# The first expert step's rows picked by one-hot matrix products instead of a gather, in a two-layer transformer kernel

## The chip, the cores and the metric

The kernel runs on one core of a Trainium2 chip, in one launch, all arithmetic in float32. The metric is the device time of one execution in microseconds (us). Before the change it is 2463.87 us, the median of three runs (2461.8 to 2465.14). One further execution was recorded by the hardware profiler; all rows below come from it.

PE is the matrix engine (TensorE), DVE the vector engine, ACT the scalar engine, POOL the GpSimd engine, SP the engine that only issues transfers. Each runs its own instruction stream; they wait for each other through counting semaphores.

## What is computed

Two layers over 1024 latent tokens of width 1024. Layer 0 mixes tokens by attention and a gated linear recurrence, layer 1 by a short convolution. Both end in the same mixture of experts: a router picks, for each token, a group and two of that group's 8 experts (32 experts in all), and every token goes through its two experts. Cut to what matters here:

```
tokens = modulate(h_lat, m[3], m[4])            # h * (1 + scale) + shift, per column
g_sel  = argmax(tokens @ wg + bg)               # 4 groups
top_i  = top_2(tokens @ we + be, inside g_sel)  # 2 of 8 experts
y      = (silu(x @ w1[e]) * (x @ w3[e])) @ w2[e]     # for each token x and each of its experts e
y_tok  = sum over the two experts of weight * y
h_lat  = layer_norm(alpha * h_lat + m[5] * y_tok)
```

`w1` and `w3` are 1024 x 512, `w2` is 512 x 1024: 6 MB per expert in float32, 192 MB per layer.

## The kernel before

**Steps and places.** How many tokens an expert gets is known only at run time. The kernel sorts the experts by load on the chip, with experts 0 and 1 always put first, and gives each a fixed *place* with a fixed capacity (`CAPS`). The places are packed into `NB` = 22 *steps* of up to 128 rows (`STEPS`). Step 0 holds places 0 and 1, which are experts 0 and 1 with 64 rows each, so its weights are known before routing; step 1 holds places 16 and 17, whose experts are known only from the routing result (`order`). Assignments beyond the capacities go to a run-time loop after the 22 steps, which stays empty if there are none.

**One step.** Its 128 token rows are fetched from memory (`h_rows`) by an indirect transfer issued by POOL (`gather`), transposed on PE in 8 blocks (`gathered_T`), and evicted with the modulation applied, four blocks by ACT and four by DVE. Then PE forms the two hidden products, `w1` in `hidden_half(b, 0)` and `w3` in `hidden_half(b, 1)`, transposes the gated result in 4 blocks (`gated_T`), and forms the product with `w2` (`output`). DVE multiplies by the gate, and POOL scatters the rows back to memory. A float32 product stands as two records each in the trace, a transpose as one.

**The PE order.** Work of neighbouring steps is interleaved, so that evictions run beside products: hidden products of step b, gated transposes of step b-1 between their halves, then the transposes of step b+1, then the output product of step b-1. The rows of steps 0 and 1 are transposed together before the first hidden product.

**Weights.** SP loads the 192 pieces of a layer (1 MB each: matrix m, half h, place q) in the fixed order `PIECES` into 16 slots, 12 of them in the array bigA and four in bigC. A piece waits until the piece that held its slot has been used for the last time; `freed` says when that is and so in which order slots are given out. The first 12 pieces need no routing result beyond the logits. Piece 12 (`PREFETCH`) and later ones wait for `order`, and slots 12 to 15 lie where the token rows `hh` were, so they also wait until these have been stored. Piece 14 waits until the first gathered rows have landed.

**Routing.** After the last logits (`select` and `count` on DVE), PE and DVE work in turn. PE counts tokens per expert (lines 1049, 1050) and ranks each assignment within its expert (lines 1053, 1054, result in bank 2). DVE sorts the experts and builds the capacities (lines 1822 to 1853). PE spreads them (line 1057) and computes `order` (lines 1060, 1061). DVE computes each assignment's step and lane (lines 1858 to 1881), and then 16 pairs of one-hot matrices (lines 1884, 1885). PE multiplies these to the *table* of row numbers (line 1066). DVE makes `tok` from it (lines 1902, 1904), and POOL may gather.

Of the kernel before, what the change touches and what calls it, by code (L numbers as in the profile page):

```python
# [13 lines left out]
P = 128  # L14
# [39 lines left out]
def freed(piece):  # L54
    m, h, q = piece
    return (LAST[q], 2 * m + h) if m < 2 else (LAST[q] + 1, 4)
# [84 lines left out]
def program(nc, T, out):  # L141
# [5 lines left out]
    with ctx:  # L147
# [192 lines left out]
        lane_is = at(bigB, 2048, 16, P)  # L340
        step_is = at(bigB, 6784, 16, TABLE)
# [32 lines left out]
        def run_over(eng, l, block_):  # L374

            eng.wait_ge(S("routed"), 6 * l + 6)
# [66 lines left out]
        def _(sp):  # L443
# [91 lines left out]
            def piece(l, n):  # L535
# [8 lines left out]
                if n == AFTER_ROUTER:  # L544
                    sp.wait_ge(S("route_mm"), 7 * l + 2)
# [38 lines left out]
            for l in range(DEPTH):  # L584
# [14 lines left out]
                sp.wait_ge(S("routed"), 6 * l + 6)  # L599
# [58 lines left out]
        def _(pe):  # L658
# [387 lines left out]
            def moe(l):  # L1046

                pe.wait_ge(S("routed"), 6 * l + 1)
                mm(bank(3)[:, 0:NE], cc("ones"), ahead[:, NT, :], start=True, stop=True, skip_group_check=True)
                mm(bank(3)[0:NE, NE:NE + 4], ahead[:, NT, :], cc("ones")[:, 0:4], start=True, stop=True,  # L1050
                   skip_group_check=True).then_inc(S("route_mm"), 1)
# [4 lines left out]
                pe.wait_ge(S("routed"), 6 * l + 2)  # L1056
                mm(bank(4)[:, 0:3 * NE], cc("ones")[0:NE, :], rows4[:, 0:3 * NE], start=True, stop=True)\
                    .then_inc(S("route_mm"), 1)
                pe.wait_ge(S("routed"), 6 * l + 3)
                mm(bank(0)[0:1, 0:NE], cc("expert")[0:NE, :], re32[2][0:NE, :], start=True, stop=True, skip_group_check=True)  # L1060
                mm(bank(0)[0:1, NE:2 * NE], cc("ones")[0:NE, 0:1], rows4[:, 3 * NE:], start=True, stop=True,
                   skip_group_check=True).then_inc(S("route_mm"), 1)

                for c in range(16):
                    pe.wait_ge(S("spot"), l * 16 + c + 1)
                    last = mm(bank(1)[:, 0:TABLE], lane_is[:, c, :], step_is[:, c, :], start=(c == 0), stop=(c == 15))
                last.then_inc(S("route_mm"), 1)
# [6 lines left out]
                def hidden_half(b, m):  # L1074

                    j = b % 2
                    if m == 0:
                        if b == 1:
                            pe.wait_ge(S("u_ev"), 2 * NTC - 2 + l + 1)
                            pe.wait_ge(S("u_ev_d"), 2 + l + 1)  # L1080
                        else:
                            pe.wait_ge(S(f"xT_ev{l}"), max(2 * b, 2))
# [19 lines left out]
                def output(b):  # L1102
# [29 lines left out]
                def block_of(i, j):  # L1132

                    b = 2 * i + j
                    pe.wait_ge(S(f"xT_ev{l}"), 2 * b)
# [6 lines left out]
                    gathered_T(b + 1, 1 - j, i + j + 1)  # L1142
# [93 lines left out]
        def _(act):  # L1236
# [137 lines left out]
            def moe(l):  # L1374
# [16 lines left out]
                rows_T(0, 0)  # L1391
                rows_T(1, 1, 6, "u_ev")
                for b in range(NB):
                    if b:
                        act.wait_ge(S(f"g_d{l}"), b)
                    silu(b)
                    if b:
                        gated(b - 1)
                        rows_T(b + 1, (b + 1) % 2)
# [70 lines left out]
        def _(dve):  # L1470
# [283 lines left out]
            def select(l, lo, hi):  # L1754

                n = hi - lo
                dve.wait_ge(S("route_mm"), 7 * l + (1 if lo == 0 else 2))
# [40 lines left out]
            def moe(l):  # L1798
# [21 lines left out]
                dve.wait_ge(S("route_mm"), 7 * l + 3)  # L1820
# [36 lines left out]
                dve.wait_ge(S("route_mm"), 7 * l + 5)  # L1857
# [3 lines left out]
                rank = bank(2)[:, 0:256].rearrange("p (t e) -> p t e", t=NT)  # L1861
# [20 lines left out]
                V.wait()  # L1882
                for c in range(16):
# [3 lines left out]
                dve.wait_ge(S("route_mm"), 7 * l + 6)  # L1887
                incl = re32[0]
                V(v.tensor_copy(incl[0:1, :], bank(0)[0:1, NE:2 * NE]))
                v.tensor_copy(order[0:1, :], bank(0)[0:1, 0:NE]).then_inc(S("routed"), 1)  # L1890
# [10 lines left out]
                dve.wait_ge(S("route_mm"), 7 * l + 7)  # L1901
                V(v.tensor_scalar(rows_of, bank(1)[:, 0:TABLE], float(ROWS), None, ADD))
# [42 lines left out]
                rows_T(0, 0)  # L1945
                rows_T(1, 1, 6, "u_ev_d")
                for b in range(NB):
                    if b:
                        gated(b - 1)
                    gate_up(b)  # L1950
                    if b:
                        rows_T(b + 1, (b + 1) % 2)
# [110 lines left out]
        def _(pool):  # L2063
# [74 lines left out]
            def moe(l):  # L2138

                pool.wait_ge(S("routed"), 6 * l + 5)  # L2140
# [13 lines left out]
                gather(0, tok[:, 0:1])  # L2154
# [66 lines left out]
```

## Time and profile before

| what | value |
|---|---|
| median of three runs | 2463.87 us |
| the profiled execution's own time | 2463.27 us |
| its span, first to last instruction | 2461.4 us |
| PE busy | 2313.6 us (94%) |
| DVE, ACT, POOL busy | 768.4, 418.8, 280.7 us |
| moved by the transfers | 572.28 MB |

The span leaves 1.9 us of the execution's time outside. The two expert parts run from about 803 to 1311 us and from about 1887 to 2394 us of the span. In a row of the timeline a first number is the start in us from the span's start, a second the time until the group's last instruction ended. Matmuls overlap, so a group's rate is read from its length and its count, not from one instruction's time. Line numbers are those of the kernel before.

### The profile page before, as it was taken

To read this page: it belongs to the slowest core of one execution; us is meant where nothing else is said; L and a number is where in the kernel's file an instruction comes from. 1 tells how busy PE (TensorE), PEld (TensorE's weight loads), DVE (VectorE), ACT (ScalarE), POOL (GpSimd) and SP (SyncE) were. 2 spreads that over 40 slices of the span, in tenths; PEclk is the share of its full clock that TensorE was granted. 3 is DMA by queue.
4 is the path that set the end of the run, shared out by engine and by line. 5 is a ranking of instruction groups with operands and counts; after the bars stand their busy time and mean duration, and the time that the engine had idled before them with its cause. 6 is when DMAs were issued, how large, how long until landed. Compare 5 with 4: busy or idle time off the path is not lost.

```text
span 2461.4 us, 28375 instructions
## 1 busy us (share of the span) xinstructions
PE 2313.6 (94%) x10444; PEld 1164.1 (47%) x10444; DVE 768.4 (31%) x1753; ACT 418.8 (17%) x912; POOL 280.7 (11%) x341
## 2 busy tenths in 40 slices
PE   6989999999996999999998999999996999999987
PEld 3546547888554344443333444444553444443332
DVE  3694114555537111111113511111345111111115
ACT  1301233444121101110102200000111101110111
POOL 0000103223122100000000000000232000000000
PEclk9999999999997999999999999999996999999999
DMA  9881000000316999999897210102207999999986
GB/s 386 297 349 58 0 1 1 2 19 19 125 55 257 387 419 414 418 413 409 357 418 278 87 51 26 51 26 88 91 35 298 419 419 416 419 407 410 374 346 256
DMA packets 146797, 572.28 MB, mean 232 GB/s; under 512 B 25033, under 2 KB 50793, under 8 KB 103914
## 3 DMA queue, kind: packets, MB, share of 16 engines
q1 hardware_dynamic: 133418, 536.97, 55.1%
q0 software_dynamic: 13248, 33.57, 3.6%
q8 instruction: 81, 1.33, 0.2%
q14 instruction: 50, 0.41, 0.0%
HBM read 549.51 MB, written 35.65 MB: 238 GB/s over the span
## 4 chain that ended last, share of the span: by engine, by line
PE 81%; DMA 7%; DVE 6%; SPq 2%; issue 2%; POOL 1%; ACT 1%; DVEq 0%; POOLq 0%; ACTq 0%
PE bank L1091 23%; PE bank L1165 13%; PE bank L1113 11%; PE bank L707 8%; PE bank L1014 4%; PE bank L974 4%; PE bank L664 3%; PE bank L810 3%; DVE lnwb L1525 2%; DMA bigA<-in_moe_w 2%; PE bank L1194 2%; SPq L445 2%; PE bank L824 1%; PE bank L793 1%; DMA bigC<-in_moe_w 1%
## 5 line engine op out<-in xcount | busy, mean ns | idle before, releaser
L1091 PE MATMUL bank<-bigA,bigB 128*32 128x512 f32 (+2 forms) x2048 | 524.9, 596 | 0.0
L1165 PE MATMUL bank<-bigB,bigA 128*128 128x512 f32 x768 | 331.6, 595 | 2.0 <-ACT bigB L1244 2.0
L1091 PEld LDWEIGHTS bank<-bigA,bigB 128*32 128x32 f32 (+2 forms) x2048 | 187.1, 141 | 299.1 <-issue 297.0
L707 PE MATMUL bank<-bigC,bigB 128*128 128x512 f32 (+3 forms) x768 | 292.4, 536 | 0.0
L1113 PE MATMUL bank<-bigA,bigB 128*32 128x512 f32 (+2 forms) x992 | 259.2, 612 | 14.8 <-DMA bigA<-in_moe_w 11.8
L1165 PEld LDWEIGHTS bank<-bigB,bigA 128*128 128x128 f32 x768 | 146.5, 191 | 186.6 <-issue 186.6
L707 PEld LDWEIGHTS bank<-bigC,bigB 128*128 128x128 f32 x768 | 142.4, 192 | 127.6 <-issue 119.5
L1244 ACT ACTIVATE bigB<-bank,small 128x128 f32<-128x128 f32 x288 | 107.5, 460 | 381.7 <-PE bank L664 381.7
L1091 PE MATMUL bank<-bigC,bigB 128*32 128x512 f32 (+2 forms) x640 | 163.2, 594 | 0.0
L1113 PEld LDWEIGHTS bank<-bigA,bigB 128*32 128x32 f32 (+2 forms) x992 | 91.4, 143 | 142.3 <-issue 138.2
L2150 POOL DMA_INDIRECT y_rows<-bigB,ints x44 | 44.5, 1011 | 909.0 <-DVE bigB L1936 909.0
L1936 DVE TENSOR_TENSOR bigB<-bank,gate 128x512 f32<-128x512 f32 x88 | 56.7, 686 | 266.6 <-PE bank L1113 266.6
L1927 DVE TENSOR_TENSOR bigB<-bigB,bank 128x512 f32<-128x512 f32 x44 | 30.3, 688 | 303.8 <-PE bank L1091 303.8
L1385 ACT ACTIVATE bigB<-bank 128x512 f32<-128x512 f32 x44 | 26.3, 597 | 555.1 <-PE bank L1091 555.1
L974 PE MATMUL bank<-bigB,bigA 128*128 128x512 f32 x256 | 112.9, 595 | 1.9 <-DMA bigB<-in_w_out_odd 1.9
L2134 POOL TENSOR_TENSOR bigC<-bigC,lnwb 128x1024 f32<-128x1024 f32 x16 | 37.6, 2352 | 617.2 <-PE bank L664 617.2
L1931 DVE COPY bigB<-bank 128x256 f32<-128x256 f32 x44 | 18.7, 424 | 263.9 <-PE bank L1099 263.9
L2031 DVE TENSOR_TENSOR bigA<-bank,bigA 128x512 f32<-128x512 f32 x16 | 11.1, 693 | 266.0 <-ACT bigA L1458 266.0
L1525 DVE SCALAR_TENSOR_TENSOR lnwb<-bigA,normw,lnwb 128x1024 f32<-128x1024 f32 x70 | 89.9, 1284 | 9.8 <-DMA bigA<-in_ada_w 5.6
L1113 PE MATMUL bank<-bigC,bigB 128*32 128x512 f32 (+2 forms) x352 | 92.2, 594 | 0.6 <-DMA bigA<-in_moe_w 0.6
L810 PE MATMUL bank<-bigB 128*128 128x128 f32 x608 | 83.8, 284 | 7.6 <-issue 6.6
L1483 DVE TENSOR_SCALAR bigB<-bank,small 128x128 f32<-128x128 f32 x224 | 76.5, 404 | 30.2 <-PE bank L664 27.2
(286 smaller groups left out, 2279.7 us busy)
## 6 DMA issues: line engine op xcount, KB each, us to landing
bigA<-in_moe_w SPq DMA_DIRECT2D x292, 1024.0 KB, 20.6
bigC<-in_moe_w SPq DMA_DIRECT2D x92, 1024.0 KB, 22.9
bigA<-in_ada_w SPq DMA_DIRECT2D x40, 1024.0 KB, 7.4
bigA<-y_rows SPq DMA_DIRECT2D x16, 1024.0 KB, 4.9
bigA<-in_w_in_odd SPq DMA_DIRECT2D x24, 512.0 KB, 6.2
bigA<-in_ada_w SPq DMA_DIRECT2D x4, 2048.0 KB, 12.5
bigC<-in_w_in_even SPq DMA_DIRECT2D x4, 2048.0 KB, 14.3
h_rows<-bigC SPq DMA_DIRECT2D x16, 512.0 KB, 4.8
```

The lines of the kernel that those rows point to most:

```text
L664: last = tp(bank(b + k // 4)[:, (k % 4) * P:(k % 4 + 1) * P], cols(src, n)[:, k, :], ident)
L707: last = mm(bank(n % 3)[:, 0:w], uT[:, k, t * P:(t + 1) * P], wring[:, g % 2, k, at_:at_ + w], start=(k == 0), stop=(k == KC - 1))
L810: last = mm(dst, sc[:, p % 3, g, k * P:(k + 1) * P], unit_p[:, p % 2, g, :], start=True, stop=True, skip_group_check=True)
L974: last = mm(bank(2 * (t % 2) + n), zT[:, k, t * P:(t + 1) * P], wout1[:, k, n * 512:(n + 1) * 512], start=(k == 0), stop=(k == KC - 1))
L1014: last = mm(bank(2 * (t % 2) + n), lhs[:, k, :], wout[k0 + k][:, n * 512:(n + 1) * 512], start=(k0 + k == 0), stop=(k0 + k == KC - 1), ski ...
L1091: last = mm(bank(m)[at_:at_ + w, :], xT[:, j, KC // 2 * h + k, at_:at_ + w], w13_at(SLOT_OF[m, h, q][0], k), start=(h == 0 and k == 0), st ...
L1113: last = mm(bank(6 + n)[at_:at_ + w, :], gT[:, 2 * h + k, at_:at_ + w], w2_at(SLOT_OF[2, h, q][0], k)[:, n * 512:(n + 1) * 512], start=(h ...
L1165: last = mm(bank(3 * half + m), wc[:, j, m, k, :], u1T[:, k, half * 512:(half + 1) * 512], start=(k == 0), stop=(k == KC - 1))
L1244: last = go(dst[k], bank(b + k // 4)[:, (k % 4) * P:(k % 4 + 1) * P], ACT.Identity, bias=shift[:, k:k + 1], scale=scale[:, k:k + 1])
L1483: last = v.tensor_scalar(dst[k], bank(b + 1)[:, (k - 4) * P:(k - 3) * P], scale[:, k:k + 1], shift[:, k:k + 1], MUL, ADD)
L1525: V(v.scalar_tensor_tensor(acc[:, r % 2], part, cond[:, k, 0:1], acc[:, r % 2], MUL, ADD))
L1936: v.tensor_tensor(yo[:, j, n * 512:(n + 1) * 512], bank(6 + n), gate[:, 1, n * 512:(n + 1) * 512], MUL)\
```

## The change

Step 0's rows are no longer gathered. Once the ranks are known, DVE takes, for each token and for experts 0 and 1, the rank plus one where the token chose the expert (`first_key`, 128 x 16), and compares it with 1 to 64. This gives a 128 x 1024 matrix of zeros and ones (`first_is`). PE multiplies the token rows `hh`, still on chip, with it: 8 column blocks by 8 token tiles, 64 products of 128 x 128. The result is the transposed rows of step 0. ACT alone evicts it, in two halves.

- PE: the rank products come first. The capacities' spread product stands after block 4 of the new products, the products for `order` after them. The table products stand between the two hidden halves of step 0. Step 0 is finished, output product included, before step 1 begins; the transposes of step 1's rows stand between the halves of step 0's output product.
- DVE: the two new operations come before the sorting of the experts; `order` is copied before the one-hot pairs.
- SP: piece 12 also waits for the new products (they read `hh`, where slots 12 to 15 lie); piece 14 no longer waits for gathered rows. `freed` says that the `w2` pieces of step 0 are free within step 0, and slots are given out accordingly.
- POOL: gathers step 1's rows first, then step 2's.

```diff
 def freed(piece):
-    return (LAST[q], 2 * m + h) if m < 2 else (LAST[q] + 1, 4)
+    return (LAST[q], 2 * m + h) if m < 2 else (LAST[q] + (LAST[q] > 0), 4)
@@ SP, piece
                 if n == PREFETCH:
-                    sp.wait_ge(S("routed"), 6 * l + 4)
+                    sp.wait_ge(S("routed"), 7 * l + 5)
                     sp.wait_ge(S("h_out"), 16 * NT * (l + 1))
-                if n == PREFETCH + 2:
-                    sp.wait_ge(S(f"xg_in{l}_0"), 16)
+                    sp.wait_ge(S(f"x_T{l}"), 1)
@@ PE, moe
+                pe.wait_ge(S("routed"), 7 * l + 2)
+                for k in range(KC):
+                    for t in range(NT):
+                        if k == 0:
+                            pe.wait_ge(S("ln"), 2 * l * NT + t + 1)
+                        last = mm(bank(6 + k // 4)[:, (k % 4) * P:(k % 4 + 1) * P], cols(hh[:, t])[:, k, :], first_is[:, t, :],
+                                  start=(t == 0), stop=(t == NT - 1), skip_group_check=True)
+                    if k == 3:
+                        last.then_inc(S("route_mm"), 1)
+                    if k == 4:
+                        pe.wait_ge(S("routed"), 7 * l + 3)
+                        mm(bank(4)[:, 0:3 * NE], cc("ones")[0:NE, :], rows4[:, 0:3 * NE], start=True, stop=True)\
+                            .then_inc(S("route_mm"), 1)
+                last.then_inc(S(f"x_T{l}"), 1)
...
-                gathered_T(0, 0, 1)
-                gathered_T(1, 1, 1, 6)
-                for b in range(NB):
+                hidden_half(0, 0)
+                table()
+                hidden_half(0, 1)
+                gated_T(0)
+                output(0)
+                for b in range(1, NB):
                     hidden_half(b, 0)
-                    if b:
+                    if b >= 2:
                         gated_T(b - 1)
                     hidden_half(b, 1)
-                    if b:
-                        gathered_T(b + 1, (b + 1) % 2, (b + 1) // 2 + 1)
+                    gathered_T(b + 1, (b + 1) % 2, (b + 2) // 2)
+                    if b >= 2:
                         output(b - 1)
@@ PE, output
+                        if b == 0 and h == 1:
+                            gathered_T(1, 1, 1)
@@ ACT, moe
-                rows_T(0, 0)
-                rows_T(1, 1, 6, "u_ev")
+                act.wait_ge(S("route_mm"), 8 * l + 5)
+                modulated(parts(xT[:, 0]), 6, mod_of(l, 1), f"xT_ev{l}")
+                act.wait_ge(S(f"x_T{l}"), 1)
+                modulated(parts(xT[:, 0]), 6, mod_of(l, 1), f"xT_ev{l}", 4, KC)
...
@@ DVE, moe
+                dve.wait_ge(S("route_mm"), 8 * l + 3)
+                V(v.scalar_tensor_tensor(first_key.rearrange("p (t e) -> p t e", t=NT), rank[:, :, 0:2], 1.0,
+                                         chosen.rearrange("p (t e) -> p t e", t=NT)[:, :, 0:2], ADD, MUL))
+                V.wait()
+                v.tensor_tensor(first_is[:, :, :].rearrange("p t (e s) -> p (t e) s", e=2),
+                                wide(cc("iota")[:, 1:65].unsqueeze(1), [P, 2 * NT, 64]),
+                                wide(first_key.unsqueeze(2), [P, 2 * NT, 64]), ALU.is_equal).then_inc(S("routed"), 1)
...
@@ POOL, moe
-                gather(0, tok[:, 0:1])
                 gather(1, tok[:, 1:2])
+                gather(0, tok[:, 2:3])
```

How this moves PE's instructions is seen in its order in layer 0, from the last logits product to step 2's first hidden products. Before (L1049 to L1054 count and rank, L1057 to L1061 spread and order, L1066 the table, L664 transposes of gathered rows, L1091 hidden products, L1099 gated transposes; in layer 0 the steps' w2 products are L1113):

```order
L962 MATMUL bank<-bigB,bigA 128x36 x8
L1049 MATMUL bank<-bigB,cst 128x32
L1050 MATMUL bank<-cst,bigB 32x4
L1053 MATMUL bank<-bigB,cst 128x256
L1054 MATMUL bank<-bigB,cst 128x224
L1057 MATMUL bank<-bigB,cst 128x96
L1060 MATMUL bank<-bigB,cst 1x32
L1061 MATMUL bank<-bigB,cst 1x32
L1066 MATMUL bank<-bigB 128x50 x16
L664 MATMUL bank<-cst,bigB 128x128 x16
L1091 MATMUL bank<-bigA,bigB 64x512 x32
L1091 MATMUL bank<-bigC,bigB 64x512 x16
```

The same place after the change (L1050, L1051 rank, L1063 the new products, L1069 spread, L1073 and L1074 order, L1102 hidden, L1081 the table):

```order
L1050 MATMUL bank<-bigB,cst 128x256
L1051 MATMUL bank<-bigB,cst 128x224
L1053 MATMUL bank<-bigB,cst 128x32
L1054 MATMUL bank<-cst,bigB 32x4
L1063 MATMUL bank<-bigB,bigC 128x128 x40
L1069 MATMUL bank<-bigB,cst 128x96
L1063 MATMUL bank<-bigB,bigC 128x128 x24
L1073 MATMUL bank<-bigB,cst 1x32
L1074 MATMUL bank<-bigB,cst 1x32
L1102 MATMUL bank<-bigA,bigB 64x512 x16
L1081 MATMUL bank<-bigB 128x50 x16
L1102 MATMUL bank<-bigA,bigB 64x512 x16
```

64 products stand where PE had a few small ones, the spread product has 40 of them ahead of it, and the table has moved behind half of step 0's hidden work. What follows there after the change, behind step 0's gated transposes (L1126 is the output product, L664 the transposes of step 1's and then step 2's rows):

```order
L1126 MATMUL bank<-bigA,bigB 64x512 x8
L664 MATMUL bank<-cst,bigB 128x128 x8
L1126 MATMUL bank<-bigA,bigB 64x512 x8
L1102 MATMUL bank<-bigC,bigB 64x512 x16
L1102 MATMUL bank<-bigA,bigB 64x512 x16
L664 MATMUL bank<-cst,bigB 128x128 x8
L1102 MATMUL bank<-bigA,bigB 128x512 x8
```

Step 2's transposes are followed at once by step 2's hidden products; step 0's output product, which stood between them before, now comes earlier.

## Rows read from the trace of the kernel before

**Rows 1.** The chain of waits in time, both layers: start us, us, what.
```profile
795.91 7.60 DMA bigB<-h_rows,ints
...
1878.83 8.12 DMA bigB<-h_rows,ints
```

**Rows 2.** Timeline of layer 0's routing: start us, us, engine, line, operation, [idle before <-releaser].
```profile
777.88 0.64 PE L1049 MATMUL bank<-bigB,cst 128*128 128x32 f32 x2 [5.93 <-DVEq L1813]
...
778.65 1.22 PE L1053 MATMUL bank<-bigB,cst 128*128 128x256 f32 x2
...
779.66 0.95 PE L1054 MATMUL bank<-bigB,cst 128*128 128x224 f32 x2
...
782.54 0.26 DVE L1858 COPY bigB<-bank 128x96 f32<-128x96 f32 x1 [0.40 <-PE bank L1057]
...
787.46 7.07 PE L1066 MATMUL bank<-bigB 128*128 128x50 f32 x32 [4.66 <-DVE bigB L1885]
...
793.58 0.17 DVE L1890 CAST ints<-bank 1x32 int32<-1x32 f32 x1
...
794.76 10.94 SPq L445 DMA_DIRECT2D bigC<-in_moe_w  x4
794.80 0.19 DVE L1904 TENSOR_SCALAR ints<-ints 128x50 int32<-128x50 int32 x1
...
803.55 3.68 PE L664 MATMUL bank<-cst,bigB 128*128 128x128 f32 x16 [9.03 <-DMA bigB<-h_rows,ints]
805.56 1.51 ACT L1244 ACTIVATE bigB<-bank,small 128x128 f32<-128x128 f32 x4 [27.28 <-PE bank L664]
```

**Rows 3.** PE's timeline through the first steps of layer 0.
```profile
807.16 15.16 PE L1091 MATMUL bank<-bigA,bigB 128*64 128x512 f32 x64
822.16 7.03 PE L1091 MATMUL bank<-bigC,bigB 128*64 128x512 f32 x32
829.12 0.75 PE L1099 MATMUL bank<-cst,bigB 128*128 128x128 f32 x4
...
844.92 7.13 PE L1091 MATMUL bank<-bigA,bigB 128*128 128x512 f32 x16
```

**Rows 4.** Line 664 between 803 and 840 us: durations min/median/max in ns.
```profile
L664 PE MATMUL bank<-cst,bigB x24: 273/417/478, 803.6 to 837.7; 128*128 128x128 f32 x24
```

**Rows 5.** The page's groups of DVE: busy us, mean ns of one, idle before.
```profile
L1927 DVE TENSOR_TENSOR bigB<-bigB,bank 128x512 f32<-128x512 f32 x44 | 30.3, 688 | 303.8 <-PE bank L1091 303.8
...
L1931 DVE COPY bigB<-bank 128x256 f32<-128x256 f32 x44 | 18.7, 424 | 263.9 <-PE bank L1099 263.9
...
L1525 DVE SCALAR_TENSOR_TENSOR lnwb<-bigA,normw,lnwb 128x1024 f32<-128x1024 f32 x70 | 89.9, 1284 | 9.8 <-DMA bigA<-in_ada_w 5.6
```

**Rows 6.** Stretches: length, busy us of PE, PEld, DVE, ACT, POOL, PEclk, DMA share, GB/s.
```profile
791.00:795.00 4.00, 3.52 (x17) 3.35 (x16) 3.86 (x24) 0.00 (x0) 0.00 (x0) 0.50 0.08 35
...
791.00:815.00 24.00, 14.97 (x65) 9.22 (x66) 8.87 (x36) 4.30 (x9) 13.63 (x20) 0.61 0.69 245
815.00:930.00 115.00, 115.00 (x508) 47.33 (x508) 18.24 (x39) 12.70 (x31) 8.13 (x8) 1.00 1.02 419
...
808.00:812.00 4.00, 4.00 (x18) 1.32 (x16) 0.64 (x2) 2.06 (x4) 2.04 (x2) 0.79 0.99 366
...
1874.00:1898.00 24.00, 14.56 (x65) 9.14 (x66) 8.87 (x36) 4.29 (x9) 13.48 (x20) 0.63 0.67 240
...
1890.00:1893.00 3.00, 3.00 (x14) 1.19 (x14) 1.74 (x6) 2.78 (x7) 2.53 (x4) 0.72 0.98 404
```

**Rows 7.** PE's timeline: waits for weights in layer 0 and layer 1.
```profile
1183.70 6.00 PE L1113 MATMUL bank<-bigA,bigB 128*32 128x512 f32 x32 [4.47 <-DMA bigA<-in_moe_w]
...
2013.75 0.62 PE L1113 MATMUL bank<-bigA,bigB 128*32 128x512 f32 x2 [0.25 <-DMA bigC<-in_moe_w]
```

**Rows 8.** Line 2145, all 48 gathers: from issue to landing.
```profile
DMA to landing us min/median/max: 4.5/10.5/11.3
```

**Rows 9.** Line 445, transfers of SP between 760 and 1320 us: the same.
```profile
DMA to landing us min/median/max: 4.9/20.5/31.8
```

More of the change, by code:

```diff
@@ L1046, in moe @@
             def moe(l):
[L1048 to L1051, printed above, removed]
+                pe.wait_ge(S("routed"), 7 * l + 1)
                 rank = bank(2)[:, 0:NT * NE]
@@ L1055, in moe @@
                     .then_inc(S("route_mm"), 1)
[L1056 to L1061, printed above, removed]
-                   skip_group_check=True).then_inc(S("route_mm"), 1)
@@ L1064, in moe @@
[L1064 to L1067, printed above, removed]
+                mm(bank(3)[:, 0:NE], cc("ones"), ahead[:, NT, :], start=True, stop=True, skip_group_check=True)
+                mm(bank(3)[0:NE, NE:NE + 4], ahead[:, NT, :], cc("ones")[:, 0:4], start=True, stop=True,
+                   skip_group_check=True).then_inc(S("route_mm"), 1)
@@ new lines, in moe, with table @@
+                last.then_inc(S(f"x_T{l}"), 1)
+                pe.wait_ge(S("routed"), 7 * l + 4)
+                mm(bank(5)[0:1, 0:NE], cc("expert")[0:NE, :], re32[2][0:NE, :], start=True, stop=True, skip_group_check=True)
+                mm(bank(5)[0:1, NE:2 * NE], cc("ones")[0:NE, 0:1], rows4[:, 3 * NE:], start=True, stop=True,
+                   skip_group_check=True).then_inc(S("route_mm"), 1)
+                def table():
+                    for c in range(16):
+                        pe.wait_ge(S("spot"), l * 16 + c + 1)
+                        last = mm(bank(4)[:, 0:TABLE], lane_is[:, c, :], step_is[:, c, :], start=(c == 0), stop=(c == 15))
+                    last.then_inc(S("route_mm"), 1)
@@ L1389, in gated @@
                     go(gT[:, 0:2, :].rearrange("p k i -> p (k i)"), bank(4)[:, 0:256], ACT.Copy).then_inc(S(f"gT_ev{l}"), 1)
-                rows_T(0, 0)
-                rows_T(1, 1, 6, "u_ev")
-                for b in range(NB):
-                    if b:
-                        act.wait_ge(S(f"g_d{l}"), b)
+                act.wait_ge(S("route_mm"), 8 * l + 5)
+                modulated(parts(xT[:, 0]), 6, mod_of(l, 1), f"xT_ev{l}")
+                act.wait_ge(S(f"x_T{l}"), 1)
+                modulated(parts(xT[:, 0]), 6, mod_of(l, 1), f"xT_ev{l}", 4, KC)
+                silu(0)
+                gated(0)
+                rows_T(1, 1)
+                for b in range(1, NB):
+                    act.wait_ge(S(f"g_d{l}"), b)
                     silu(b)
-                    if b:
+                    if b >= 2:
                         gated(b - 1)
-                        rows_T(b + 1, (b + 1) % 2)
+                    rows_T(b + 1, (b + 1) % 2)
                 gated(NB - 1)
@@ L1882, in moe @@
                 V.wait()
+                dve.wait_ge(S("route_mm"), 8 * l + 7)
+                incl = re32[0]
+                V(v.tensor_copy(incl[0:1, :], bank(5)[0:1, NE:2 * NE]))
+                v.tensor_copy(order[0:1, :], bank(5)[0:1, 0:NE]).then_inc(S("routed"), 1)
                 for c in range(16):
@@ L1943, in scattered @@
                     output(b % 2)
[L1945 to L1948, printed above, removed]
+                gate_up(0)
+                gated(0)
+                rows_T(1, 1)
+                scattered(0)
+                for b in range(1, NB):
+                    if b >= 2:
                         gated(b - 1)
                     gate_up(b)
-                    if b:
-                        rows_T(b + 1, (b + 1) % 2)
+                    rows_T(b + 1, (b + 1) % 2)
+                    if b >= 2:
                         scattered(b - 1)
@@ L2160, in moe @@
                 for b in range(NB):
-                    pool.wait_ge(S(f"x_T{l}"), b + 1)
-                    gather(b % 2, tok[:, b + 2:b + 3])
                     if b:
+                        pool.wait_ge(S(f"x_T{l}"), b + 1)
+                        gather(b % 2, tok[:, b + 2:b + 3])
                         pool.wait_ge(S(f"y_ev{l}"), 2 * b)
```

43 lines of the change are left out of this document (18 added, 25 removed).

## The prediction

> **What bounds the kernel now.** I read the busy shares first. PE is busy 94% of the span, so PE's empty stretches and its slow stretches are what a change can win. Then I read the chain of waits in time: in both expert parts it runs through the gather of step 0's rows, 7.60 us in layer 0 and 8.12 us in layer 1 [rows 1]. The timeline around it shows that PE has little to do for some 25 us while the routing is worked out [rows 2]. Its ranking products end at 780.61 (779.66 + 0.95), the table products take 7.07 us at the pace of DVE's one-hot matrices, and PE then waits 9.03 us for the rows. From 807.16 on PE runs without a gap [rows 3]. This empty time is what the change tries to use.
>
> The second view is the stretches. The transfers stay at 419 GB/s from 815 to 930 us, while PE is busy 115.00 of 115 us [rows 6]. Both resources are full, and the waits for weights show how closely they are matched: 4.47 us at 1183.70 in layer 0, and already 0.25 us at 2013.75 in layer 1, five steps in [rows 7]. So I keep two accounts per layer: when PE reaches step 2, and how many bytes the transfers are behind. The layer shifts by the later of the two.
>
> **PE's account, layer 0.**
> - Ranking products: they ran from 778.65 to 780.61, behind two short ones [rows 2]. Now they go first, at 777.88, and end at 779.84.
> - DVE's two new operations: the first is 128 x 16, 0.2 us (the 1 x 32 copy took 0.17 [rows 2]). The second makes 128 x 1024. A 128 x 1024 operation with three operands took 1.28 us and one of 128 x 512 0.69 us [rows 5]; these are its ends, and since it is full width I take 1.2. With the handovers the new products start at 781.4.
> - The 64 products are 128 records, with a strided 128 x 128 stationary block and 128 columns, as in the transposes of line 664. Sixteen such records took 3.68 us at the low clock and one alone 0.42 [rows 2, 4], so a record takes (3.68 - 0.42) / 15 = 0.217 us at 1.2 GHz and half, 0.109 us, at 2.4 GHz.
> - How many run slowly: after 803.55 PE was busy with transposes and then hidden products, and the clock's mean of 0.79 in 808 to 812 puts the rise at 809.7, 6.1 us later. In layer 1 the transposes began when the rows landed (1886.95), and a mean of 0.72 in 1890 to 1893 puts it at 1891.7, 4.7 us later [rows 1, 6]. I take 5.2 us: 24 records slow, 104 fast: 5.2 + 11.3 = 16.5. The spread product between them and the last one's tail add 0.6. The rows of step 0 are there at 798.5. The ends are 24 records at the fast rate (2.6 us less) and all 128 at the slow rate (11.2 us more).
> - ACT evicts the second half in 1.51 us [rows 2], the first half being hidden behind the products. Step 0's first hidden half starts at 800.2, where before it started at 807.16.
> - First half 7.0 (to 807.2). The table's 32 records are ready: DVE's spread copy can start at 793.3 (spread product behind 80 records), the 4.4 us to the one-hots (782.54 to just before 787.46) end at 797.7. They wait for `order`'s copies at 799.3 and take 6.6 us, to 805.9. Table at 0.109 each: 3.6, to 810.8. Second half 7.0, to 817.8.
> - Here work that overlapped now stands in series: DVE's gate product 0.69, four transposes 0.75, a copy 0.42 [rows 3, 5], with handovers 2.2, to 820.0. Output product 7.0 with step 1's transposes of 1.0 within it, to 828.0. Hidden of step 1: 14.0, to 842.0.
> - Then the transposes of step 2's rows (1.05) are followed at once by its hidden products, which must wait for the eviction: 1.51 and two handovers, 1.6. Before, step 0's output product covered this. Step 2 starts at 844.65, against 844.92 [rows 3]: 0.3 us earlier.
>
> So nearly all of the gain of 7 us at the start is spent: 3.6 on table products that used to cost PE nothing, 2.2 on the gating in series, 1.6 on the uncovered eviction. The 16.5 us of new products sit where PE was idle.
>
> At the clock the Trainium skill ("TensorE: Matmul & The Clock Gate", "Part 1: The HAM clock gate") says that the clock is low by default and sustained matmul activity releases it. The trace agrees for the transposes, but not for the table products: PE had worked on them since 787.46 and was busy 3.52 of 4 us from 791 to 795, and the granted clock stood at 0.50 [rows 2, 6]. If the rule held for any stream of matmuls, the clock would have been up by then; so it alone does not promise that the new products are fast, and this gives the third rival.
>
> **The transfers' account.** From 791 to 815 they ran at 245 GB/s, short of 419 by 24 x (1 - 245/419) = 10.0 us [rows 6]: the wait for `order`, then piece 14's wait for the gathered rows, then the slots of step 0. Now piece 12 waits for `order`, whose products stand behind the 128 records: 798.5, 0.5 for them, 0.3 for the two copies, 1.0 to SP's issue (793.75 to 794.76 before [rows 2]), so 800.3, 5.5 us later than before. A piece lands 4.9 us after its issue at the least [rows 9], of which 2.5 is 1 MB at 419 GB/s; I put the first byte 1.3 us after the issue (ends 0 and 2.4). The transfers then stand empty from 791 to 801.6, less the 0.3 us of traffic up to 795: 10.3. After that nothing stops them: slots of step 0's `w1` come free at 803.7 and 807.2, while four pieces last to 811.6; the eight pieces that wait for step 0's hidden products and the two gathers last to 834; the `w2` slots of step 0 come free at 828. The gather of step 0's rows is gone, 0.52 MB or 1.25 us. Net: 10.3 - 10.0 - 1.25 = 1.0 us ahead. Layer 1, with 240 GB/s [rows 6], gives the same.
>
> **Sum.** Layer 0 goes by PE: -0.3. In layer 1 the wait of 0.25 us goes too: -0.55. All later waits for weights move with it, since their pieces' slots are freed by PE and the order of the rest is the same. The profiled execution took 2463.27, so 2462.4; the median of the runs lies 0.6 above it, so I say 2463. Other work is as before: POOL's 16 scalings and DVE's list of overflow blocks stay beside PE.
>
> **The rivals.**
> 1. *Faster: the slow part of the new products is shorter.* For it: PE is busy from 777.88 on, with a rest of only 1.5 us before the new products, while it had waited 9.03 us ahead of the transposes that came before the rise [rows 2]. Against: the table products, 7 us of them, had no effect. With all 128 records fast both accounts gain 2.6 us a layer: 2463 - 5 = 2458.
> 2. *Slower: step 1's rows come too late.* The table ends at 810.8, `tok` is made at 811.3, POOL issues 0.9 later as before (794.99 to 795.91 [rows 1, 2]), at 812.2. At the median of 10.5 us the rows land at 822.7, at the maximum of 11.3 at 823.5 [rows 8], and PE wants them at 823.5, in the middle of step 0's output product. It decides from 11.3 us on. The second gather follows at once and the queue holds eight pieces; before, the first gathers had emptier queues and took 7.60 [rows 1]. At 14 us PE waits 2.7 us a layer: 2468 to 2469.
> 3. *Slower: the clock stays at 1.2 GHz* through the new products: step 0's rows, `order` and piece 12 come 11 us later, in both accounts and layers: 2463 + 22 = 2485.
> 4. *The weights don't keep up*, so that the change does not do what it says for them: if the shortfalls after piece 12's issue stay (10.0 less 4.7 before it, so 5 us), the transfers are 4 us behind in each layer and PE waits for it at the fifth step: 2471.
>
> **Chances.** Forecast 0.50 (its own range 2459 to 2467), rival 1 0.20, rival 2 0.16, rival 3 0.06, rival 4 0.08. The measurement cannot tell less than 0.2%, 4.9 us, from no change. Faster by more: 0.13 of rival 1 and 0.07 of the forecast's cases, where the work in series is shorter than I count, 0.20. Slower by more: rivals 3 and 4, 0.14, 0.06 of rival 2, whose centre lies near the bound, and 0.04 of the forecast's: 0.24. Same: 0.56. The range 2456 to 2472 leaves out rival 3 and the edges.
>
> **What would show it.** In the profile after: 128 records of line 1063 in 16 to 18 us from 781.4, at 0.22 us and later 0.11; step 0's hidden products at 800.2; a gap of about 1 us before the gated transposes, one of some 1.6 us before step 2's hidden products; none in the middle of step 0's output product; piece 12 at 800.3 and then 419 GB/s without a break; step 2 at 844.7. The forecast is wrong if the low clock lasts beyond 791, if PE waits for a gather in step 0, or if the first wait for weights at the fifth step grows.

## The result, and the profile after

| | us |
|---|---|
| before, median of 4 runs | 2462.84 (2460.5 to 2465.14) |
| after, median of 4 runs | 2492.36 (2489.71 to 2496.41) |
| ratio after to before | 1.0121, 95% interval 1.0104 to 1.0139 |
| forecast | 2463, range 2456 to 2472 |

The kernel after is 29.5 us slower, and outside the range. Its profiled execution took 2492.48 us. The span grew by 29.2 us, PE's busy time by 49.6 (from 2313.6), the transfers' bytes fell by 0.32 MB. From the page of after:

```profile
span 2490.6 us, 28859 instructions
...
PE 2363.2 (95%) x10684; PEld 1214.0 (49%) x10684; DVE 768.5 (31%) x1749; ACT 421.8 (17%) x920; POOL 278.7 (11%) x339
...
DMA packets 146511, 571.96 MB, mean 230 GB/s; under 512 B 24830, under 2 KB 50590, under 8 KB 103626
```

PE's timeline in layer 0 answers to [rows 2, 3] (line numbers of after: 1063 are the new products, 1081 the table, 1102 hidden, 1126 output):

```profile
778.00 1.22 PE L1050 MATMUL bank<-bigB,cst 128*128 128x256 f32 x2 [5.93 <-DVEq L1833]
...
781.50 19.36 PE L1063 MATMUL bank<-bigB,bigC 128*128 128x128 f32 x80 [1.06 <-DVE bigB L1845]
800.79 0.46 PE L1069 MATMUL bank<-bigB,cst 32*128 32x96 f32 x2
801.17 11.71 PE L1063 MATMUL bank<-bigB,bigC 128*128 128x128 f32 x48
...
814.48 8.78 PE L1102 MATMUL bank<-bigA,bigB 128*64 128x512 f32 x32 [1.40 <-ACT bigB L1260]
823.19 3.77 PE L1081 MATMUL bank<-bigB 128*128 128x50 f32 x32
826.89 7.09 PE L1102 MATMUL bank<-bigA,bigB 128*64 128x512 f32 x32
834.84 0.75 PE L1110 MATMUL bank<-cst,bigB 128*128 128x128 f32 x4 [0.86 <-DVE bigB L1954]
836.11 3.65 PE L1126 MATMUL bank<-bigA,bigB 128*64 128x512 f32 x16 [0.52 <-DVE bigB L1958]
...
860.87 1.55 PE L1102 MATMUL bank<-bigA,bigB 128*128 128x512 f32 x3 [1.60 <-ACT bigB L1260]
```

The new products start where I said (781.50 for 781.4) and end at 812.9 instead of 798.5. Their 80 + 48 = 128 records take 19.36 + 11.71 = 31.1 us, 0.24 each (31.0 in layer 1). Everything behind them moves with them: step 0 starts at 814.48 (forecast 800.2), step 2 at 860.87 (844.65). The instructions of line 1063 (count, then min/median/max ns):

```profile
L1063 PEld LDWEIGHTS bank<-bigB,bigC x256: 312/336/338, 781.5 to 1911.0; 128*128 128x128 f32 x128
L1063 PE MATMUL bank<-bigB,bigC x256: 344/402/606, 781.5 to 1911.1; 128*128 128x128 f32 x128
```

Loading one stationary block (LDWEIGHTS) takes 336 ns, where the contiguous 128 x 128 blocks of line 1091 before take 190. Did the clock cause it? The stretches of after answer to [rows 6] (columns as there):

```profile
781.00:788.00 7.00, 6.50 (x27) 6.50 (x28) 3.39 (x22) 0.00 (x0) 0.00 (x0) 0.50 1.00 390
788.00:795.00 7.00, 7.00 (x32) 7.00 (x31) 0.00 (x0) 0.00 (x0) 0.00 (x0) 1.00 0.45 190
...
791.00:815.00 24.00, 22.60 (x100) 21.85 (x101) 5.86 (x24) 3.57 (x9) 0.00 (x0) 1.00 0.01 5
815.00:930.00 115.00, 112.03 (x509) 47.08 (x506) 25.63 (x75) 12.55 (x30) 18.75 (x25) 0.99 1.01 414
```

No. The granted clock rose from 0.50 to 1.00 at 788, 6.5 us after the products' start (I had assumed 5.2), but the count of records went only from 27 in 6.5 us to 32 in 7 us. The counts include records that cross an edge; the last 48 records, all at 1.00, took 11.71 us, 0.244 each. In layer 1 the clock rose 3.6 us after the start, and the products took the same 31.0 us. The third row shows the transfers: 5 GB/s from 791 to 815, where before had 245 [rows 6]. The later waits for weights are there again, 15.7 us later, of the same length: 1199.39 with 4.50 us for 1183.70 with 4.47 [rows 7].

### The profile page after: what moved, and what is told of

Its sections match the earlier page's. It is cut to its first block, busy times and chain, and to the rows that moved or that the text cites. A ratio compares the mean times of both kernels' runs of the same rounds, so it can differ in the third digit from the quotient of the medians.

```text
span 2490.6 us, 28859 instructions
## 1 busy us (share of the span) xinstructions
PE 2363.2 (95%) x10684; PEld 1214.0 (49%) x10684; DVE 768.5 (31%) x1749; ACT 421.8 (17%) x920; POOL 278.7 (11%) x339
## 4 chain that ended last, share of the span: by engine, by line
PE 83%; DMA 6%; DVE 4%; SPq 3%; issue 2%; ACT 1%; POOL 1%; DVEq 0%; ACTq 0%; POOLq 0%
PE bank L1102 22%; PE bank L1181 13%; PE bank L1126 11%; PE bank L707 8%; PE bank L1014 4%; PE bank L974 4%; DMA bigA<-in_moe_w 3%; PE bank L810 3%; PE bank L664 3%; PE bank L1063 2%; SPq L447 2%; DVE lnwb L1545 2%; PE bank L1210 2%; DMA bigA<-in_ada_w 1%; PE bank L824 1%
## 5 line engine op out<-in xcount | busy, mean ns | idle before, releaser
L1102 PE MATMUL bank<-bigA,bigB 128*32 128x512 f32 (+2 forms) x1888 | 426.2, 596 | 6.0 <-ACT bigB L1260 6.0
L1126 PE MATMUL bank<-bigA,bigB 128*32 128x512 f32 (+2 forms) x1120 | 274.1, 610 | 14.1 <-DMA bigA<-in_moe_w 13.0
L1102 PE MATMUL bank<-bigC,bigB 128*128 128x512 f32 (+2 forms) x800 | 283.6, 594 | 0.0
L1102 PEld LDWEIGHTS bank<-bigA,bigB 128*32 128x32 f32 (+2 forms) x1888 | 146.1, 134 | 222.2 <-issue 213.7
L1126 PEld LDWEIGHTS bank<-bigA,bigB 128*32 128x32 f32 (+2 forms) x1120 | 97.0, 140 | 153.3 <-issue 150.1
L1102 PEld LDWEIGHTS bank<-bigC,bigB 128*128 128x128 f32 (+2 forms) x800 | 101.6, 153 | 142.3 <-issue 142.1
L810 PEld LDWEIGHTS bank<-bigB 128*128 128x128 f32 x608 | 72.7, 191 | 17.5 <-issue 15.0
```

What stands on the lines that cost most here:

```text
L810: last = mm(dst, sc[:, p % 3, g, k * P:(k + 1) * P], unit_p[:, p % 2, g, :], start=True, stop=True, skip_group_check=True)
L1102: last = mm(bank(m)[at_:at_ + w, :], xT[:, j, KC // 2 * h + k, at_:at_ + w], w13_at(SLOT_OF[m, h, q][0], k), start=(h == 0 and k == 0), st ...
L1126: last = mm(bank(6 + n)[at_:at_ + w, :], gT[:, 2 * h + k, at_:at_ + w], w2_at(SLOT_OF[2, h, q][0], k)[:, n * 512:(n + 1) * 512], start=(h ...
```

## The experiments

Ratios are to runs of the kernel before taken beside each: 2463.82 us (median of 22) for e1_unit, e3_rows_first and e_no_hold, 2462.95 us (median of 25) for the three e6 kernels. A *step* is the distance between neighbouring elements of an operand, in float32 elements of 4 bytes; step 1 is contiguous.

**m1_strides: what makes a record slow.**
```
for i in range(32): mm(dst(i), strided(i, 8), wide[:, 0:P], ...)     # steps 1, 2, 4, 8, 16
```


> A kernel of its own that only measures: streams of 32 float32 matmuls (64 records) with 128 moving columns, which differ in the step between the elements of the stationary 128 x 128 block (1, 2, 4, 8, 16 elements), one with step 8 that goes round four accumulation regions instead of filling one after the other, one with step 8 in the moving operand alone, 32 transposes with step 8, and 16 matmuls of 512 columns with stationary step 8 and step 1. No other engine works in the meantime. Theory A (the strided stationary operand is slow to load): contiguous 0.11 us a record, step 8 0.24 in both accumulation orders, 0.11 for the transposes and for the strided moving operand; with 512 columns 0.24 or less, so no loss. Theory B (what is slow is the accumulation of 8 matmuls in a row in the same 128 columns of PSUM): the contiguous stream has 0.24 as well, the one that goes round has 0.11. Theory C (another engine's reading or writing of SBUF or PSUM slowed the new products): all at 0.11.

One execution. Its profile gives full clock throughout; the opening stream of 512-column products was slow at first even so (64 records in 30.6 us, later 27.6), but no row below is from that stretch. Groups by line: 59 has stationary step 1, 63 step 2, 67 step 4, 71 and 75 step 8 (75 round four regions), 79 step 16, 83 step 8 in the moving operand, 87 the transposes, 91 and 93 512 columns with step 8 and 1. Busy us, mean ns, idle before:

```profile
L75 PE MATMUL bank<-wide,big 128*128 128x128 f32 x64 | 15.3, 400 | 0.0
L71 PE MATMUL bank<-wide,big 128*128 128x128 f32 x64 | 15.3, 400 | 0.0
L83 PE MATMUL bank<-big,wide 128*128 128x128 f32 x64 | 15.1, 412 | 0.0
L67 PE MATMUL bank<-wide,big 128*128 128x128 f32 x64 | 15.0, 395 | 0.0
L79 PE MATMUL bank<-wide,big 128*128 128x128 f32 x64 | 14.0, 380 | 0.0
L91 PE MATMUL bank<-wide,big 128*128 128x512 f32 x32 | 13.9, 592 | 0.0
L93 PE MATMUL bank<-wide,big 128*128 128x512 f32 x32 | 13.9, 592 | 0.0
L63 PE MATMUL bank<-wide,big 128*128 128x128 f32 x64 | 7.7, 281 | 0.0
L59 PE MATMUL bank<-wide,big 128*128 128x128 f32 x64 | 7.3, 275 | 0.0
...
L87 PE MATMUL bank<-eye,big 128*128 128x128 f32 x32 | 3.7, 275 | 0.0
```

Busy time over count is the pace: 0.114 us at step 1, 0.120 at step 2, 0.234 at step 4, 0.239 at step 8 in either order, 0.219 at step 16, 0.117 for the strided transposes. Theory A holds for the stationary operand; B (accumulation in place) and C (another engine) fall. Its claim for the moving operand fell: strided it costs the same 0.236. With 512 columns the slow load is hidden, 0.43 either way.

**e1_unit: the same in the kernel.** One operand differs; it brings other columns of the rows.
```
- cols(hh[:, t])[:, k, :]
+ hh[:, t, k * P:(k + 1) * P]
```


> The kernel after, with the stationary operand of the new products taken from 128 columns that lie side by side instead of every eighth one; it brings the wrong columns of the rows, everything else is as before. Theory A (load of the strided block): the 128 records take 16 to 17 us instead of 31, step 0's hidden products start at 800 and step 2's at 846 instead of 861; the total falls by 2 x 14.4 = 29 us, to 2463 to 2465. Theory B (accumulation) and C (contention with DVE's work beside it): no change, 2492. Theory D (the 29 us are lost in waits for gathered rows or weights and not in the products): the products get faster and the total stays above 2480.

2465.15 us, ratio 1.001 (1.0 to 1.0019): 1.3 of the 29.5 us are left, which the interval hardly tells from nothing. PE's timeline; this execution reached the first ranking product at 776.10, 1.9 us earlier than after's:

```profile
779.59 10.77 PE L1063 MATMUL bank<-bigB,bigC 128*128 128x128 f32 x80 [1.06 <-DVE bigB L1845]
...
790.68 5.62 PE L1063 MATMUL bank<-bigB,bigC 128*128 128x128 f32 x48
...
797.89 7.09 PE L1102 MATMUL bank<-bigA,bigB 128*64 128x512 f32 x32 [1.39 <-ACT bigB L1260]
804.91 3.77 PE L1081 MATMUL bank<-bigB 128*128 128x50 f32 x32
...
842.58 3.70 PE L1102 MATMUL bank<-bigA,bigB 128*128 128x512 f32 x8 [1.59 <-ACT bigB L1260]
```

The 128 records take 16.4 us (forecast 16.5), and 17.2 in layer 1. Theory A is shown in place, and D (waits for rows or weights) falls.

**e3_rows_first: the product turned round.** The right rows without a strided load: the one-hot matrix is stationary, the rows are moving.
```
for n in range(2):
    for t in range(NT):
        mm(bank(6 + n), first_is[:, t, :], hh[:, t, n * 512:(n + 1) * 512], ...)
# ACT copies to first_rows, then 8 transposes of cols(first_rows)
```


> The kernel after with the products turned round: the one-hot matrix is the stationary operand (its elements lie side by side) and the rows of the layer norm are the moving one, 16 matmuls of 512 columns give the 128 rows, ACT copies them to SBUF, and 8 transposes as for the other steps follow. Theory A: 16 matmuls take 13.7 us at the high clock and some 16 us with the first 5 at the low one, the copy 0.7, the transposes 1, the eviction 1.5: step 0's hidden products start at 801 instead of 814.5, and the total is 2492.4 less 2 x 13.5, so 2464 to 2467. Theory D: above 2480. If the records of the rows of the one-hot are paced at 0.24 each in the low clock until the end, 2475.

2464.95 us, ratio 1.001 (1.0001 to 1.002). The theory's time came out; the start of step 0 did not, 803.36 for 801, because ACT alone evicts all eight blocks: PE waited 3.00 us. Step 2 starts 71.2 us after the first routing product, 4.7 later than in e1, and yet the total is the same. What PE waited for weights later in layer 0, first in e1, then in e3 (total us, times, longest):

```profile
PE bank L1126 <- DMA bigA<-in_moe_w: 7.9, 4, 4.5
```
```profile
PE bank L1130 <- DMA bigA<-in_moe_w: 3.8, 1, 3.8
```

PE came 4.7 us later and waited 4.1 us less. This was new: PE's account does not decide the layer here.

**e_no_hold: the change at piece 14 alone.** The kernel before without
```
- if n == PREFETCH + 2: sp.wait_ge(S(f"xg_in{l}_0"), 16)
```


> The kernel before, with one thing taken out: the weights' piece 14 does not wait for the gathered rows of step 0 any more. It isolates the second half of the change's few words. The transfers of pieces 14 and 15 then run some 4 us earlier and beside the two gathers, whose rows may land later (7.6 us before, in an emptier queue). My forecast's two accounts: PE's account cannot gain, since only the rows of step 0 hold it up, 2463; if the gathers land 1 to 3 us later, 2465 to 2469; the transfers' gain of 1 to 4 us shows in the wait at the fifth step (4.47 us) only where PE does not start later.

2467.88 us, ratio 1.0029 (1.0017 to 1.0041). The timeline of PE (lines as in before, less 3):

```profile
802.68 1.97 PE L661 MATMUL bank<-cst,bigB 128*128 128x128 f32 x8 [9.59 <-DMA bigB<-h_rows,ints]
806.47 1.97 PE L661 MATMUL bank<-cst,bigB 128*128 128x128 f32 x8 [1.81 <-DMA bigB<-h_rows,ints]
808.37 15.26 PE L1088 MATMUL bank<-bigA,bigB 128*64 128x512 f32 x64
```

Where before had one wait of 9.03 us [rows 2], there are two; the gathered rows now land beside four pieces of weights instead of two. From the first routing product, step 0's hidden products start after 31.9 us instead of 29.3. So the hold in before was worth some 4 us over both layers. In after no gather stands at this place; whether a hold would be worth anything there was not tried.

**e6_early, e6_late, e6_table: which account binds.** From e3, with the order changed around the rows. The core of the edit is below; besides, DVE shares copy and eviction with ACT and copies `order` earlier, and the transposes of step 2's rows stand between the halves of step 1's hidden products.
```
for t in range(NT):                       # tile by tile, both halves of the columns
    mm(bank(6), first_is[:, t, :], hh[:, t, 0:512]); mm(bank(7), first_is[:, t, :], hh[:, t, 512:])
    if t % 2: last.then_inc(S("rows_mm"), 1)
    if t == 0: spread and order products
table(0, 5); transposes; table(5, 11); hidden_half(0, 0); table(11, 16); hidden_half(0, 1)
# SP:      if 12 <= n < 16: wait_ge(S("rows_mm"), 4 * l + n - 11)
# e6_late:                  wait_ge(S("rows_mm"), 4 * l + 4)
# e6_table: table(5, 16) ahead of hidden_half(0, 0)
```


> The products turned round as in e3, and all around them reordered: the rows are made tile by tile (both halves of a tile at once), so that pieces 12 to 15 of the weights each wait for two tiles only; the spread and order products stand behind the first tile; DVE shares the copy and the eviction with ACT; 11 of the 16 table products stand in PE's gaps between the rows, the transposes and step 0; the transposes of step 2's rows stand inside step 1's hidden products, as cover for their eviction. Before, after with contiguous operand (e1) and e3 end layer 0 within 0.3 us of each other, counted from the first ranking product, though step 2 starts 66.5 to 71.2 us after it. So by theory E (transfers bind: the layer's length follows from when the stream of weights runs without a hole) the hole from 791 to 801 shrinks to 4 to 6 us and each layer ends 3 to 4 us earlier: 2456 to 2458. By theory F (PE binds) step 2 is reached 2 to 3 us earlier than before, and the total is 2458 to 2460; nothing gained where neither binds: 2463.

> e6 with one difference: pieces 12 to 15 all wait for the last tile's products. PE's program is the same. Theory E (transfers bind): piece 12 is issued some 10 us later and the hole is 9 to 10 us again, as in e3, so the gain of e6 goes: 2463 to 2465. Theory F (PE binds): as e6, 2458 to 2460, since each of these pieces still lands before step 1 needs it.

> e6 with the last five table products also ahead of step 0's hidden products. Step 0, and with it the first slots that come free, is 1.2 us later, the gather of step 1's rows is issued some 7 us earlier. Theory E: 1 us a layer longer than e6, 2 in all; theory F: the same as e6 within 0.5 us; if in e6 PE waits for step 1's rows in the output product of step 0, up to 2 us a layer shorter.

Measured: e6_early 2458.01, ratio 0.998 (0.997 to 0.999); e6_late 2463.36, ratio 1.0003 (0.9994 to 1.0012); e6_table 2457.47, ratio 0.9977 (0.9968 to 0.9986). SP's timeline (first row of each) and the stretch from 788 to 808 us, first of e6_early, then of e6_late:

```profile
787.58 10.30 SPq L448 DMA_DIRECT2D bigC<-in_moe_w  x4
...
788.00:808.00 20.00, 19.68 (x89) 9.92 (x87) 10.52 (x50) 3.88 (x7) 0.00 (x0) 1.00 0.77 275
```

```profile
797.71 3.76 SPq L448 DMA_DIRECT2D bigC<-in_moe_w  x4
...
788.00:808.00 20.00, 19.68 (x90) 9.96 (x88) 10.36 (x49) 3.98 (x7) 0.00 (x0) 1.00 0.56 223
```

PE is busy 19.68 of 20 us in both, and step 2 starts 64.2 and 64.0 us after the first routing product. Only SP's waits differ: pieces 12 to 15 are issued 10.1, 8.2, 5.9 and 3.6 us earlier in e6_early. With that go 275 or 223 GB/s, which is 1.04 MB over 20 us or 2.5 us at 419 GB/s; layer 0 is 2.4 us shorter, and the total by 5.4 us in the medians. e6_early alone lies on the border of what E and F gave; e6_late is where E put it (2463 to 2465) and not where F did (2458 to 2460). Theory E, transfers bind, is shown by the pair; F falls. In e6_table the gathers' issue moved from 810.09 to 802.45, but the total agrees with e6_early's within the intervals: the 1 us a layer that E expected is not seen.

One view sets all runs side by side, the rate of the transfers over 60 us from the first routing product. Layer 1 of before, after, e_no_hold and e6_early:

```profile
1860.91:1920.91 60.00, 44.75 (x204) 23.48 (x206) 21.99 (x94) 6.36 (x15) 13.48 (x20) 0.74 0.83 321
```
```profile
1876.64:1936.64 60.00, 56.17 (x259) 42.84 (x259) 19.79 (x86) 5.61 (x13) 11.15 (x18) 0.94 0.56 221
```
```profile
1862.16:1922.16 60.00, 41.71 (x186) 21.77 (x188) 21.13 (x92) 6.21 (x14) 13.45 (x20) 0.71 0.76 297
```
```profile
1855.82:1915.82 60.00, 57.24 (x248) 25.93 (x250) 25.86 (x101) 8.29 (x19) 14.49 (x21) 0.94 0.91 345
```

The table has, for layers 0 / 1, that rate, step 2's start in layer 0, and the layer's length, up to the start of the last step's output product (1303.99 in before), all counted from the first routing product:

| kernel | GB/s | step 2 | length, us |
|---|---|---|---|
| before | 344 / 321 | 67.0 | 526.1 / 524.7 |
| after | 239 / 221 | 82.9 | 541.8 / 539.3 |
| e1_unit | 342 / 320 | 66.5 | 525.9 / 524.3 |
| e3_rows_first | 332 / 314 | 71.2 | 526.1 / 524.5 |
| e_no_hold | 323 / 297 | 69.8 | 529.0 / 526.5 |
| e6_early | 361 / 345 | 64.2 | 522.8 / 521.3 |
| e6_late | 348 / 315 | 64.0 | 525.2 / 526.4 |
| e6_table | 366 / 335 | 63.5 | 522.4 / 523.5 |

Where the two columns part, the lengths go with the first: in e3 step 2 is 4.2 us later than in before and layer 0 as long. In after both are late, so its own length does not tell them apart. An estimate from the first column, for after in layer 0: 105 GB/s less over 60 us are 6.3 MB, at 419 GB/s 15.0 us; less 1.25 for the gather that is gone, 13.8; measured 15.7. For e_no_hold 21 GB/s are 3.0 us; measured 2.9. For e6_early 17 GB/s are 2.4, and the gather 1.25: 3.7; measured 3.3. The others come within 1 us in layer 0. In layer 1 the estimate misses by up to 2.2 us, most in e6_late and e6_table, which are that much longer than it gives. In these two executions PE was slower there as well: in e6_late the granted clock stood at 0.50 from 1863 to 1870 where e6_early had 0.75 from 1859 to 1866, and step 0's hidden products started 25.9 us after the first routing product (26.6 in e6_table, whose order of the table products is part of it) instead of 23.4. So layer 0 is the clean comparison of the pair. The clock does not make the 5.4 us of the medians: its mean over an execution is 0.977 to 0.980 in all runs of both kernels.

**m2_strides: what the first left open.**
```
for i in range(64): mm(dst(i), strided(i, 8), wide[:, 0:P], ...)       # first stream, on an idle TensorE
... step 3; the identity as other operand; moving step 8 with 512 columns
```


> Second measuring kernel, for what the first left open: the strided products at the low clock (the first stream, 128 records with stationary step 8, starts on an idle TensorE), a step of 3 elements, whether the identity as the other operand makes a strided matmul as fast as a transpose (32 matmuls with the strided block stationary and the identity moving, and 32 the other way round), transposes of contiguous blocks, and 16 matmuls of 512 columns with step 8 in the moving operand. If the pace of 0.24 us comes from reading the strided block of SBUF, it is the same at both clocks and with the identity, step 3 lies between 0.12 and 0.24, and the moving operand of 512 columns, which it must read in full, takes 0.9 us or more a record instead of 0.43. If the pace comes from TensorE itself, it is 0.48 at the low clock. A transpose of a contiguous block takes the same 0.117 as that of a strided one.

One execution. PE's timeline (56: step 8, first stream; 60: step 3; 64: step 8 stationary, identity moving; 68: the reverse; 72: transposes of contiguous blocks; 76: 512 moving columns with step 8; 78: contiguous):

```profile
16.43 30.79 PE L56 MATMUL bank<-wide,big 128*128 128x128 f32 x128 [16.43 <-DMA eye<-in_const_e]
...
53.92 11.26 PE L60 MATMUL bank<-wide,big 128*128 128x128 f32 x64
...
71.89 15.27 PE L64 MATMUL bank<-eye,big 128*128 128x128 f32 x64
...
93.86 15.09 PE L68 MATMUL bank<-big,eye 128*128 128x128 f32 x64
...
115.65 3.66 PE L72 MATMUL bank<-eye,big 128*128 128x128 f32 x32
...
126.02 29.54 PE L76 MATMUL bank<-big,wide 128*128 128x512 f32 x32
155.38 13.92 PE L78 MATMUL bank<-wide,big 128*128 128x512 f32 x32
```

Step 3 gives 0.176, the identity changes nothing (0.239 and 0.236), and 512 strided moving columns take 0.92 us a record against 0.43, the 0.9 expected if the read sets the pace. These fit a pace set by the reading of the strided block. The first stream, which began on an idle engine, has 0.2405 a record. The profile gives full clock there, but its records differ. Line 56 from 16 to 20 us and from 26 to 40 us (count, then min/median/max ns):

```profile
L56 PE MATMUL bank<-wide,big x15: 442/449/604, 16.4 to 20.0; 128*128 128x128 f32 x15
```
```profile
L56 PE MATMUL bank<-wide,big x61: 401/402/403, 25.6 to 39.9; 128*128 128x128 f32 x61
```

In after the records of line 1063 have a median of 444 ns while the granted clock is 0.50 and 402 at 1.00. By that likeness the opening of this stream ran at the low clock too, and its 15 records in 3.58 us have the same pace, 0.24. Still open is why a transpose does not pay: contiguous 0.114, strided 0.117.

## Why the prediction was wrong

**The step that failed** is the term of the 64 new products: "The 64 products are 128 records, with a strided 128 x 128 stationary block and 128 columns, as in the transposes of line 664." The count and the start were right, the clock's rise roughly (6.5 and 3.6 us after the start for 5.2); the price was not. I took 0.217 us at 1.2 GHz and 0.109 at 2.4 from strided *transposes* [rows 2, 4]. A strided *product* takes 0.24 at either, so the term of 16.5 us measured 31.1 and 31.0 in the two layers. At the low clock the price was nearly right (0.217 for 0.24); what failed is the halving. A transpose is one record and a product two, which the trace before shows; that they are different instructions should have forbidden carrying the price over. No row of before has a float32 product with a strided block of 128 columns, so by my own method the term needed a bound above. The trace of before did hold a warning: line 679's products load blocks of 64 columns with step 8, at a granted clock of 1.00, and a load takes 216 ns on the mean, where the contiguous ones of 64 columns (line 824) take 136 (the clock is at 0.56 in the 1.8 us behind them, so a low clock may have a part in this). I bounded only the clock ("all 128 at the slow rate, 11.2 us more"), and the measured term lies 3.4 us beyond even that.

The pace goes with the step in memory: 0.120 at 8 bytes, 0.176 at 12, 0.234 at 16, 0.239 at 32, and 0.219 at 64, a little less again, which is unexplained. The Trainium skill ("SBUF — State Buffer", "Door 1: The DMA port swizzle") says that SBUF is read in lines of 16 bytes and that two hits in a line are needed for full rate. The runs agree with these two statements, steps of 8 bytes being free and those of 16 bytes twice as slow; they differ from the page where it counts 4 float32 elements as still free, and it does not cover the transposes. I had not weighed it. Had the term been taken at the 0.234 a record that m1_strides measured afterwards, it would have been 30 us and the forecast some 2490.

**Point by point,** with the forecast's times moved by the 1.8 us by which e1_unit's execution reached this place earlier:
- Start of the products 781.50 for 781.4; DVE's two operations 0.17 and 1.23 us for 0.2 and 1.2. Right.
- With the price mended, e1_unit starts step 0 at 797.89 for 798.4, the table at 804.91 for 805.4, step 2 at 842.58 for 842.9, issues piece 12 at 797.90 for 798.5, and is 0.2 and 0.4 us shorter than before in the layers, for 0.3 and 0.55 (one execution each; the medians differ by 1.3 us the other way). So the terms in series (table 3.8, gating 2.1, eviction 1.6) were right, and so was the cancelling of the gain. That its products took 16.4 us for 16.5 is in part luck: a record cost 0.117 at full clock, not 0.109, and the clock rose 3.3 us after the start, not 5.2; in layer 1 it rose after 5.0 us, and they took 17.2.
- "The trace agrees for the transposes" says more than the rows: the transposes ended at 807.2, and the hidden products had run for 2.5 us when the clock rose at 809.7, so the two are not told apart.
- Rival 2 (step 1's rows late) did not happen: no wait for a gather in step 0. Rival 4 (a shortfall of the transfers after piece 12's issue) did not come either: in e1_unit they ran at 423 GB/s from 802 to 815. In after they are late because piece 12 is, issued at 814.48 for 800.3.
- Rival 3 gave 2485 for a clock that stays low, and was nearest; the mechanism was another.
- "The layer shifts by the later of the two" accounts: in e3 PE's account is 4.2 us late and the layer is not, since PE's waits for weights shrink by as much. The e6 pair shows the transfers binding where PE's times agree. My PE account said -0.3, the transfers' -1.0 in layer 0, so this changed nothing in the number; it would have shown where a better version lies.
- In layer 0 the first hidden half took 8.78 us for 7.0; the last section has it.

**The rest of the 29.5 us.** The layers are 15.7 and 14.7 us longer than before, 30.4 together; behind the last output product the execution was 1.2 us shorter. Against e1_unit, the products account for 31.1 - 16.4 = 14.7 in layer 0 and 31.0 - 17.2 = 13.8 in layer 1; the slower first half of step 0 adds up to 1.7 in layer 0.

## What to carry to other kernels

Take the price of a product from a row with the same instruction, the same operands' steps in memory and the same width; where there is none, bound it from above by a slow load of every block. Put the strided operand where it is hidden or avoid it: a product that loads a 128 x 128 block for only 128 columns has nothing to hide it behind. And where transfers and PE are both near full, first ask when the next transfer may be issued and whether the stream then runs without a hole: here four pieces issued 10 to 4 us earlier in each layer were worth 5 us of the total with PE's program unchanged, while 4.7 us of PE's time at the same place were worth nothing.

## What the runs showed of the hardware

- A float32 block of 128 x 128 whose elements lie 16 or 32 bytes apart takes 0.234 to 0.239 us a record as the stationary operand of a product of 128 columns, 0.219 at 64 bytes, against 0.114 contiguous; as the moving operand (32 bytes tried) it takes 0.236. In after the pace did not change as the clock went from 0.50 to 1.00 (0.24 at both). Behind 512 contiguous columns the slow load is hidden (0.43).
- After a wait of 1.40 us the granted clock fell again during step 0's first hidden half in layer 0 of after: the half took 8.78 us where the next took 7.09, and the clock's mean was 0.76 from 813 to 820:

```profile
813.00:820.00 7.00, 5.60 (x21) 1.75 (x20) 6.81 (x35) 2.71 (x5) 0.00 (x0) 0.76 0.64 226
```

In e1_unit and in layer 1 of after the same half, after a wait of 1.39 us, took 7.09; in e3_rows_first, after 3.00 us, it took 8.63 and 8.78. What told the two waits of 1.4 us apart was not tried.
- A wait that holds transfers of weights back until a gather has landed can be worth its time: in e_no_hold, without it, the first two gathers of layer 0 landed 8.2 and 10.4 us after their issue instead of 7.6 [rows 1] and 7.1.
